# ScalarE's order in the xm stage: silu behind the next eviction, weight split behind the silu in front

## What is computed

```python
    u = rms_norm(x, norm_g) @ w_in
...
    xm, om, gates, zm, xp, zp = jnp.split(u, [s1, s2, s3, s4, s5], axis=-1)
    xc = jax.nn.silu(causal_conv(xm, conv_w, conv_b))
...
    q = jnp.einsum('bshc,hcd->bhsd', xc_h, w_q).astype(jnp.float32)
    k = jnp.einsum('bshc,hcd->bhsd', xc_h, w_k).astype(jnp.float32) * (M_HEAD_DIM ** -0.5)
    v = jnp.einsum('bshc,hcd->bhsd', xm_h, w_v).astype(jnp.float32)
```

## Time and profile before

| | us |
|---|---|
| median of three runs | 1925.95 (1925.57 to 1927.27) |
| the profiled execution | 1929.72 |
| its span, first to last instruction | 1927.60 |
| mean granted clock of TensorE | 0.964 |
| busy: TensorE, VectorE, ScalarE, GpSimd | 1770.0, 1167.0, 977.0, 233.0 |

### The profile page before, as it was taken

How to read it: one execution, slowest core, us unless ns; L and a number is a source line. 1 busy time by engine, 2 the same in 40 slices (tenths; PEclk the granted TensorE clock), 3 DMA queues, 4 the chain that set the end, 5 groups by cost and what they waited for, 6 DMA issues and landing times.

```text
span 1927.6 us, 23396 instructions
## 1 busy us (share of the span) xinstructions
PE 1770.0 (92%) x8766; PEld 1441.4 (75%) x8766; DVE 1167.0 (61%) x1641; ACT 977.0 (51%) x1332; POOL 233.0 (12%) x174
## 2 busy tenths in 40 slices
PE   6999999999899599999999983899999998988898
PEld 6888878888788477777767763777878887877567
DVE  3543435555563799999999975652549624337453
ACT  4222234444423589998988974345333223448331
POOL 0000000000000144443323320100010000000000
PEclk9999999999999699999999996999999999999799
DMA  6756347434144799999999972322023331212001
GB/s 143 107 90 98 97 79 66 67 66 66 45 142 183 279 415 421 422 420 423 422 420 421 421 261 113 119 66 88 10 80 108 132 108 62 88 59 100 1 1 66
DMA packets 129091, 326.47 MB, mean 169 GB/s; under 512 B 8176, under 2 KB 84720, under 8 KB 120816
## 3 DMA queue, kind: packets, MB, share of 16 engines
q1 hardware_dynamic: 123408, 315.85, 49.9%
q0 software_dynamic: 5168, 8.92, 1.3%
q10 hardware_dynamic: 432, 0.56, 0.1%
HBM read 319.02 MB, written 15.21 MB: 173 GB/s over the span
## 4 chain that ended last, share of the span: by engine, by line
PE 63%; DVE 13%; DMA 9%; issue 9%; ACT 6%; DVEq 0%; POOL 0%; SPq 0%; ACTq 0%; POOLq 0%
PE bank L1358 12%; PE bank L1360 12%; PE bank L1359 12%; DMA down<-in_w_e_down 6%; PE turned L1358 3%; PE turned L1360 3%; PE turned L1359 3%; DVE down_lo L2266 3%; PE bank L1689 2%; DVE gate_lo L2266 2%; DVE up_lo L2266 2%; PE bank L1529 2%; PE bank L1434 1%; PE bank L1444 1%; ACT w_hi L868 1%
## 5 line engine op out<-in xcount | busy, mean ns | idle before, releaser
L1919 DVE TENSOR_TENSOR w_lo<-w_raw,w_hi 128x2048 fp32r<-128x2048 f32 (+2 forms) x83 | 179.5, 2164 | 340.2 <-ACT w_hi L868 340.1
L868 ACT ACTIVATE w_hi<-w_raw 128x2048 fp32r<-128x2048 f32 (+3 forms) x139 | 182.2, 1332 | 279.3 <-DMA w_raw<-in_w_in 72.8
L1358 PE MATMUL bank<-h1T_hi,w_hi 128*128 128x512 f32 x376 | 152.4, 405 | 0.0
L1360 PE MATMUL bank<-h1T_hi,w_lo 128*128 128x512 f32 x376 | 148.2, 394 | 0.0
L1359 PE MATMUL bank<-h1T_lo,w_hi 128*128 128x512 f32 x376 | 147.6, 392 | 0.0
L2266 DVE TENSOR_TENSOR down_lo<-down,down_hi 128x2048 fp32r<-128x2048 f32 x62 | 139.0, 2280 | 2.5 <-ACT down_hi L868 2.4
L2266 DVE TENSOR_TENSOR gate_lo<-gate,gate_hi 128x2048 fp32r<-128x2048 f32 x64 | 128.9, 2017 | 0.0
L2266 DVE TENSOR_TENSOR up_lo<-up,up_hi 128x2048 fp32r<-128x2048 f32 x64 | 126.5, 2019 | 1.1 <-ACT up_hi L868 1.1
L868 ACT ACTIVATE down_hi<-down 128x2048 fp32r<-128x2048 f32 x62 | 115.1, 1905 | 16.7 <-DMA down<-in_w_e_down 16.7
L868 ACT ACTIVATE gate_hi<-gate 128x2048 fp32r<-128x2048 f32 x64 | 108.7, 1700 | 19.2 <-DMA h_dram<-h_tok 9.8
L799 POOL COPY put_row<-table 64x1 int32 (+1 forms) x32 | 86.3, 2696 | 261.0 <-DVE ys L2301 258.8
(11 more groups left out here) (689 smaller groups left out, 4492.9 us busy)
## 6 DMA issues: line engine op xcount, KB each, us to landing
gate<-in_w_e_gate SPq DMA_DIRECT2D x32, 2048.0 KB, 16.9
up<-in_w_e_up SPq DMA_DIRECT2D x32, 2048.0 KB, 17.3
down<-in_w_e_down SPq DMA_DIRECT2D x32, 2048.0 KB, 18.2
w_raw<-in_w_in SPq DMA_DIRECT2D x24, 1024.0 KB, 9.0
w_raw<-in_a_w_in SPq DMA_DIRECT2D x20, 1024.0 KB, 5.2
w_raw<-in_w_in SPq DMA_DIRECT2D x16, 512.0 KB, 9.5
w_raw<-in_a_w_out SPq DMA_DIRECT2D x8, 1024.0 KB, 5.0
w_raw<-in_c_w_in SPq DMA_DIRECT2D x6, 1024.0 KB, 5.3
```

The costliest lines, as they stand in the source:

```text
L868: return nc.scalar.activation(out, in_, ACT.Copy, scale=scale)
L1358: pe.matmul(out, sh, mh, start=start, stop=False)
L1360: return pe.matmul(out, sl, mh, start=False, stop=stop)
L1919: V.tensor_tensor(ring_view(w_lo, n), ring_view(raw, n), ring_view(w_hi, n).bitcast(F32), ALU.subtract)\
```

## The change

ScalarE's instructions in the stage stand in another order. The silu of chunk j and the copy of its high part come behind the eviction of chunk j+1; the weight split of an even chunk comes behind the silu of the chunk before it (for chunk 0 straight behind its eviction), no longer behind its own silu. The last silu stands at the end of the stage, ahead of the split of the second om slice. The waits go along with their instructions. The other engines' programs are the same.

```diff
--- before.py
+++ after.py
@@ -1178,16 +1178,20 @@
             act.wait_ge(sem("r_fin_made"), 1)
             for tt in range(TT):
                 copy(x1_tok[:, tt, :], x2g_tok[:, tt, :], r_fin[:, tt:tt + 1]).then_inc(sem("x3_made"), 1)
-            for s in range(4):
-                for j in (2 * s, 2 * s + 1):
-                    evict_hi(("xm", j), xmT_hi[:, j, :])
-                    until_taken(act, ("xm", j))
-                    if j >= 2:
-                        act.wait_ge(sem("xc_lo"), j - 1)
-                    step(nc.scalar.activation(xs_t[j % 2][:, :], cv_t[j % 2][:, :], ACT.Silu))
-                    copy(xcT_hi[:, j, :], xs_t[j % 2][:, :]).then_inc(sem("xc_hi"), 1)
-                    if j == 2 * s:
-                        split(slice_no[("xm", s)] + 2, n_slices)
+            def conv_silu(j):
+                until_taken(act, ("xm", j))
+                if j >= 2:
+                    act.wait_ge(sem("xc_lo"), j - 1)
+                step(nc.scalar.activation(xs_t[j % 2][:, :], cv_t[j % 2][:, :], ACT.Silu))
+                copy(xcT_hi[:, j, :], xs_t[j % 2][:, :]).then_inc(sem("xc_hi"), 1)
+
+            for j in range(KC):
+                evict_hi(("xm", j), xmT_hi[:, j, :])
+                if j >= 1:
+                    conv_silu(j - 1)
+                if j % 2 == 0:
+                    split(slice_no[("xm", j // 2)] + 2, n_slices)
+            conv_silu(KC - 1)
             split(slice_no[("gates", 0)] + 2, n_slices)
             act.wait_ge(sem("g_abs_made"), 1)
             step(nc.scalar.activation(g_e[:, :], g_abs[:, :], ACT.Exp, scale=-1.0))
```

## The result

The changed kernel took 1917.0 us (median of four runs, 1916.64 to 1920.66) beside 1926.61 us for the kernel before (1925.57 to 1928.76), a ratio of 0.9941 with a 95% interval of 0.9926 to 0.9955. The forecast was 1913.1 us within 1911.0 to 1917.0: faster, as predicted, by 9.6 us between the medians instead of 12.8, exactly at the upper bound of the range. The ratio is not the quotient of the two medians (0.9950); by it the gain is 11.4 us, by its interval 8.7 to 14.3. In two later comparisons the same kernel had ratios of 0.9926 (0.9913 to 0.9939) and 0.9930 (0.9914 to 0.9945). The profiled execution took 1920.66 us, its span is 1918.6 us.

The account below looks back on a forecast made before the run. The ScalarE-VectorE relay, not TensorE, was taken to set the stage's end; stalls of 1.27 and 9.30, slower matmuls of 0.12 and 2.02 and a 0.10 delay make 12.8 us: 1925.95 - 12.8 = 1913.1 us, range 1911.0 to 1917.0.

Parts of the forecast that it names:

- the relay: xm stage: ScalarE and VectorE wait on each other per chunk, so a pair takes 14.87 us against TensorE's 10.88.
- The sum: TensorE's stalls, slower matmuls and small delay around gates and om slices: together 12.8 us to be gained.
- Both stalls: TensorE stops before the gates group, 1.27 us, and before the first om slice, 9.30 us; both should go.
- the low clock behind the second: First om matmuls after the 9.30 us stall: twelve distances take 4.74 us instead of 2.72, costing 2.02 us.
- the small delay ahead of the third om slice: TensorE at the third om slice, kernel before: late by 0.10 us, 0.3 at most by the table of waits.
- What is late next: After the change, the third om slice is tightest: weights done 1266.4, wanted 1268.3, 1.9 us to spare.
- The table load: ScalarE's 1.28 us load before the first silu, now behind eviction 1 with 3.5 us free: zero cost.
- GpSimd beside VectorE: GpSimd's 1.30 us low part of each silu could delay VectorE's splits 0 to 1.30 us per meeting; 0 taken.
- rival 1: Third om slice becomes late as GpSimd holds up VectorE's splits: 1913.8 to 1917.2 us, middle 1915.5; chance 0.06.
- rival 2: Later waits behind the stage give back part of the gain, up to 8.6 us: 1921.7 us; chance 0.03.
- rival 3: Engines in the xm stage still wait for each other, pair stays 14.87 us, nothing moves: 1926 us; chance 0.04.
- Rival 4: TensorE's clock falls to 1.2 GHz in the unbroken stretch from xm on; 100 slow matmuls give 1935.8; chance 0.03.

Follow-up runs that it names:

- split-only kernel: Kernel before with only the weight split of an even chunk moved right behind that chunk's eviction, silus unmoved: 1919.79 us, ratio 0.9939; stage 128.20 us.
- six-copy kernel: Changed kernel plus six unused 128x512 ScalarE copies (4.0 us) between the last silu's copy and the second om slice's split: stage 130.91 us.

## Why the prediction was right, and where it was not

- **What bounds the stage**: right. With the relay broken up, the pair of evictions takes 10.88 us, and every row on VectorE came within 0.15 us of its forecast once the later start (1.74 us) is taken off: first om slice 1241.94 - 1.74 = 1240.20 (1240.30), second 1249.43 (1249.55), third 1264.03 (1264.15), end of the last convolution 1246.2 (1246.30).
- **The sum**: 12.8 forecast, 12.89 measured in the stage, the same in all four profiles of the changed kernel. Both stalls, the low clock behind the second and the small delay ahead of the third om slice are gone.
- **The delay ahead of the third om slice**: the size was right, the row was not. The 0.3 us in the table of waits lies at the w_out products, far behind the stage, and is there after the change, too. At the third om slice the kernel before shows no idle time; its first two matmuls stand 0.31 us apart instead of 0.23, and the distance ahead of them is 0.02 too long, together the 0.10 of the sum:

```profile
1281.06 0.47 PE L1358 MATMUL bank<-w_hi,h2T_hi 128*128 128x512 f32 x1
1281.37 0.40 PE L1359 MATMUL bank<-w_lo,h2T_hi 128*128 128x512 f32 x1
...
1542.27 0.47 PE L1358 MATMUL bank<-w_hi,ya_hi 128*128 128x512 f32 x1 [0.25 <-DVE w_lo L1919]
```

- **What is late next**: right, the third om slice, with 1.86 us to spare instead of 1.9.
- **The table load, the copies behind the eviction**: free, as said.
- **GpSimd beside VectorE**: right for this change, no low part met a split, and the gates split took 1.22 us instead of 1.41. In the split-only kernel, where they do meet, the price can be read (next section).
- **Which part does it**: the prediction began its costing with "the eviction leaves the relay" and gave the split no share of its own. Of the 12.89 us, the split's move brings 11.74 alone and the silu's 3.97. With the 1.9 us split out of the way, an eviction that still stands behind the silu costs 1.15 us.
- **The step that was off**: "1925.95 - 12.8 = 1913.1" with its own range of 1.6 us either way. The measured 1917.0 lies outside of that range (1911.5 to 1914.7). It is within 1911.0 to 1917.0, by nothing to spare, only because this had been widened for rival 1, which did not happen: that part is luck. The gain in the stage is exact, but the rest of an execution moves by more than I allowed. In six profiles of the two kernels the stage starts anywhere from 1195.49 to 1202.53, and the part behind it takes 589.7 to 590.4 us where the clock stays up at the xp restart, and 592.4 where it falls. The first comparison had the stage 1.74 us late and the clock down in its profile; its median was 9.6 us lower. But that profile is of its longest run, 1920.66 us, and the other three have none, so what the median lacks is not shown to be these two losses; the interval of its ratio (8.7 to 14.3 us) holds the forecast gain anyway. The second and third had ratios that are worth 14.3 us and 13.5 us of 1926. The three average 1 - 0.9932 = 0.68%, 13 us. The spread of the runs shown, 1925.57 to 1927.27, was too few values to read it from.
- **The rivals**: none happened. TensorE had no idle row ahead of an om slice (rival 1), its waits behind the stage kept their sizes, the longest 8.63 us before and after (rival 2), the silus' waits for VectorE are gone but for the last (rival 3). The load of the v2 slice starts 71.03 us into the stage instead of 83.80, 12.8 us earlier, as forecast. Rival 4's direction, TensorE slowed by long unbroken work, did not show: 126.8 us at 1.00. The clock did take something back, but behind a wait of 2.17 us that was there before. Where the variation ahead of the stage comes from was not tried and stays open.

## What to carry to other kernels

Where two in-order engines hand a tile to and fro, the pace is the longest round through both; look for the longest instruction on that round that nobody in the round needs, and put it where its engine would wait anyway. Here that was a 1.9 us weight split, and moving it alone was worth three times as much as moving the silu alone, which looks like the cause. Check a forecast of this kind in the stage, where 0.1 us can be read, and give the whole time the spread of the rest.

## What the runs showed of the hardware

**The clock after a short stop.** Behind one and the same TensorE wait of 2.17 us the clock fell to the lower level in four of ten profiles. Some eight matmuls then stood 0.43 us apart instead of 0.227, at a cost of 1.57 us (110.91 against 109.34 us to the next wait). The 1.98 us stop of the six-copy kernel cost 1.72 us more in the same way. Behind the shorter stops ahead of gates (1.12 us, kernel before) and of the third om slice (0.86 us, split alone) the matmuls stood 0.23 us apart at once. So a stop of 2 us can cost nearly 4.

**GpSimd and VectorE on the same SBUF operands.** In the split-only kernel GpSimd's low part starts while VectorE's split (1209.63 to 1211.91, above) is at work:

```profile
1211.14 1.95 POOL L846 TENSOR_TENSOR xcT_lo<-xs_t,xcT_hi 128x512 fp32r<-128x512 f32 x1 [46.71 <-ACT xcT_hi L868]
1217.00 1.30 POOL L846 TENSOR_TENSOR xcT_lo<-xs_t,xcT_hi 128x512 fp32r<-128x512 f32 x1 [3.91 <-ACT xcT_hi L868]
```

It took 1.95 us instead of 1.30, 0.65 more for 0.77 us of overlap; two more of the eight fell so, and VectorE's split kept its 2.28 us. Where GpSimd was first, VectorE paid: 0.18 us for 0.32. The Trainium skill, in "SBUF — State Buffer" (section "SBUF: two separate sides"), has whoever starts second stand still; these rows agree in kind, and the loss is a little less than the overlap.
